# Output projections: splitting moved into the stage in front, no meeting of engines, and projection products inside the last delta head's scan

## The reference

```python
# layer 0 and 1 of the first network
y_lat = jnp.concatenate([o, fourier_mix(f)], axis=-1) @ w_out      # attention heads and Fourier groups
y_lat = hyena_mixer(...)                                           # (gate * long convolution) @ w_out
x = layer_norm(alpha * x + g1 * y_lat, ln1_g[i], ln1_b[i])
# layer 0 and 1 of the second network
y = o * lax.rsqrt(jnp.mean(o * o, axis=-1, keepdims=True) + EPS) * onorm   # gated delta rule, 8 heads
y_lat = (y.astype(z.dtype) * jax.nn.silu(z).reshape(...)).reshape(b, l, d) @ w_out
y = (gate_b * conv3_grid(gate_c * hx, conv_w, rows)) @ w_out       # short convolution
x = x + gt_m * y
```

## Time and profile before

| | us |
|---|---|
| median of 3 runs (3809.39 to 3812.03) | 3809.65 |
| profiled execution | 3807.93 |
| its span | 3806.0 |
| PE busy / DVE busy / ACT busy / POOL busy | 3340.8 / 1824.8 / 1131.5 / 428.9 |

### The profile page before, as it was taken

How to read it: one execution, slowest core, us unless ns; L and a number is a source line. 1 busy time by engine, 2 the same in 40 slices (tenths; PEclk the granted TensorE clock), 3 DMA queues, 4 the chain that set the end, 5 groups by cost and what they waited for, 6 DMA issues and landing times. The chain is left out here.

```text
span 3806.0 us, 47649 instructions
## 1 busy us (share of the span) xinstructions
PE 3340.8 (88%) x18241; PEld 2257.7 (59%) x18241; DVE 1824.8 (48%) x2900; ACT 1131.5 (30%) x1882; POOL 428.9 (11%) x428
## 2 busy tenths in 40 slices
PE   8999899899988899977999998699886996998886
PEld 6767587766755787746888886344332773433332
DVE  6774687457874877354565564311112543111112
ACT  3042443234213332345445443111111321111111
POOL 1200000001300000012233230111110000111110
PEclk7999999999989999988999998799998997999998
DMA  6340355322612355211121120699997204999995
GB/s 226 130 148 23 102 177 181 133 100 89 243 67 66 122 178 187 68 27 32 32 58 37 32 76 2 261 405 400 425 411 284 108 24 201 415 406 407 401 391 206
DMA packets 224678, 692.89 MB, mean 182 GB/s; under 512 B 28019, under 2 KB 108115, under 8 KB 199284
## 3 DMA queue, kind: packets, MB, share of 16 engines
q1 hardware_dynamic: 194016, 652.63, 45.0%
q10 hardware_dynamic: 11764, 20.97, 1.5%
q0 software_dynamic: 18720, 16.84, 1.3%
HBM read 700.78 MB, written 40.94 MB: 195 GB/s over the span
## 5 line engine op out<-in xcount | busy, mean ns | idle before, releaser
L642 PE MATMUL psum<-work_rounded 128*128 128x512 f32 (+1 forms) x2224 | 811.6, 405 | 76.9 <-DVE work_rounded L636 32.7
L642 PE MATMUL psum<-work_rounded,ring_rounded 128*128 128x512 f32 (+1 forms) x1824 | 726.9, 399 | 0.0
L642 PEld LDWEIGHTS psum<-work_rounded 128*128 128x128 f32 x2224 | 429.2, 193 | 189.6 <-issue 78.7
L3678 PE MATMUL psum<-ring,fixed 128*64 128x512 f32 x1184 | 414.7, 658 | 96.3 <-DMA ring<-in_w 55.0
L631 ACT ACTIVATE work_rounded<-ring 128x1024 fp32r<-128x1024 f32 x204 | 214.3, 1057 | 804.5 <-PE psum L642 665.5
L642 PE MATMUL psum<-fixed_rounded,work_rounded 128*128 128x512 f32 (+1 forms) x1088 | 435.6, 400 | 0.0
L642 PEld LDWEIGHTS psum<-work_rounded,ring_rounded 128*128 128x128 f32 x1824 | 353.2, 194 | 81.1
L3833 DVE TENSOR_TENSOR work<-work,psum 64x512 f32<-64x512 f32 (+1 forms) x64 | 44.2, 691 | 700.0 <-ACT work L3763 546.1
L636 DVE TENSOR_TENSOR ring_rounded<-ring,work_rounded 128x1024 fp32r<-128x1024 f32 x189 | 230.3, 1222 | 274.5 <-ACT work_rounded L631 274.5
L3678 PEld LDWEIGHTS psum<-ring,fixed 128*64 128x64 f32 x1184 | 130.9, 150 | 332.8 <-issue 332.8
L365 DVE SCALAR_TENSOR_TENSOR work<-ring,fixed,work 128x512 f32<-128x512 f32 x364 | 300.6, 835 | 25.5 <-issue 1.7
(11 more groups left out here) (408 smaller groups left out, 5022.2 us busy)
## 6 DMA issues: line engine op xcount, KB each, us to landing
ring<-in_w SPq DMA_DIRECT2D x128, 2048.0 KB, 17.1
work<-in_w SPq DMA_DIRECT2D x64, 2048.0 KB, 21.5
ring<-in_mod_w SPq DMA_DIRECT2D x24, 2048.0 KB, 8.4
ring<-in_ada_w SPq DMA_DIRECT2D x24, 2048.0 KB, 8.1
ring<-in_ffn_w_in SPq DMA_DIRECT2D x44, 1024.0 KB, 7.6
ring<-in_ffn_w_out SPq DMA_DIRECT2D x10, 2048.0 KB, 7.8
ring<-in_w_in_a SPq DMA_DIRECT2D x32, 512.0 KB, 6.6
ring<-in_hy_w_in SPq DMA_DIRECT2D x6, 2048.0 KB, 8.2
```

The lines of the kernel that those rows point to most:

```text
L642: ins = pe.matmul(out, c.rounded(w), c.rounded(x), start=(start and i == 0), stop=(stop and i == 2))
L3678: ins = pe.matmul(c.ps[64 * j:64 * j + 64, 2, :], self.gt_sb[:, k, 0:64], weights(o, j)[:, k, :], start=(k == 0), stop=(k == KD - 1))
```

## The change

The three simple stages and `DeltaHeads` are now joined, so the four barriers go. The splits of the projection stand in the stage in front: on ACT and DVE as the tiles are completed in `FourierMix`, `HyenaConv` and `ShortConv`, and on ACT and POOL in the inversion and scan of delta head 7 (its last tile on ACT and DVE). Split parts have new places, and in the delta projection four units in place of three. In `FourierMix` the turning of the heads is put ahead of the second group, and the tiles are consumed in the order 4, 0, 1, 2, 3, 5, 6, 7. In head 7, products of the output projection stand behind steps 3, 4 and 5 of the scan and around the mean over features, into PSUM banks that are free there. No arithmetic is added or taken away: the number of splits and matmuls is the same.

```diff
@@ class Project
+    def unit_in(self, act, m):
+        if m % 4 == 0:
+            self.c.arrived(act, self.n[m // 4])
+        self.parts.make_high(act, m, self.unit(m), None, 0)
+    def tile_in(self, act, q):
+        act.wait_ge(self.ready, self.ready0 + q + 1)
+        self.parts.lift(act, q)
+    def part_of_tile(self, pe, m, steps):
+        ins = self.parts.product(pe, self.bank(m), m, self.unit(m), steps, True)
@@ Project.scalar
-        c.arrived(act, self.n[0])
-        self.parts.open_high(act, self.unit(0), self.unit(1))
-        for k in range(KD):
-            self.parts.lift(act, k)
-        self.parts.make_high(act, 2, self.unit(2), None, 0)
@@ Project.vector
-        self.parts.open_low(dve, self.unit(0))
-        for k in range(KD):
-            self.parts.lower(dve, k)
-        for m in range(1, UNITS):
-            self.parts.make_low(dve, m, self.unit(m))
@@ FourierMix
-            if g == 2:
+            if g == 1:
                 self.attention.turn(pe)
...
+        project.units_in(act)
+        for g, tiles in enumerate(((0, 1, 2), (3, 4, 5), (6,), (7,))):
...
@@ HyenaConv.scalar, .vector
+            if m in (1, 2, 3):
+                self.project.unit_in(act, m - 1)
+            for q in {4: (0, 1, 2), 5: (3, 4), 6: (5,), 7: (6, 7)}.get(m, ()):
+                self.project.tile_in(act, q)
...
+            for q in {5: (0, 1, 2), 6: (3, 4), 7: (5, 6, 7)}.get(m, ()):
+                parts.lower(dve, q)
@@ ShortConv.vector
+                for q in {22: (0, 1, 2), 23: (3, 4, 5, 6, 7)}.get(j, ()):
+                    parts.lower(dve, q)
@@ DeltaHeads.gpsimd, after the eight heads
+        parts.open_low(pool, project.unit(0))
+        for m in range(1, project.count):
+            parts.make_low(pool, m, project.unit(m))
+        for q in range(DHEADS - 1):
+            parts.lower(pool, q)
@@ DeltaHeads.tensor
-        self.tensor_sums(pe, DHEADS - 1)
+        project.part_of_tile(pe, 1, range(2, last))
+        self.tensor_sums(pe, last)
+        project.part_of_tile(pe, 2, range(0, last))
+        for m in range(3):
+            project.part_of_tile(pe, m, range(last, KD))
@@ DeltaHeads.tensor_scan, at the end of a step
+            else:
+                for m, steps in {3: ((0, range(0, 2)),), 4: ((0, range(2, 5)),), 5: ((0, range(5, 7)), (1, range(0, 2)))}.get(step, ()):
+                    self.project_out.part_of_tile(pe, m, steps)
@@ DeltaHeads.scalar_invert, scalar_scan
+            if h + 1 == DHEADS and v > WHOLE - 2:
+                self.project_out.unit_in(act, v - WHOLE + 1)
...
+            if h + 1 == DHEADS and l and step < 2:
+                self.project_out.unit_in(act, 2 + step)
+            if h + 1 == DHEADS and l:
+                for q in ((0,), (1, 2), (3, 4), (5, 6), (), ())[step]:
+                    self.tile_in(act, q)
@@ stages
-            add(FourierMix(c, attention))
+            mixer = add(FourierMix(c, attention), joined=True)
-            add(HyenaConv(c))
+            mixer = add(HyenaConv(c), joined=True)
-            add(heads)
+            add(heads, joined=True)
-            mixer = add(ShortConv(c))
+            mixer = add(ShortConv(c), joined=True)
```

More of the change, by code:

```diff
@@ L710, in first_two, with product @@
         return last
-    def product(self, pe, out, u, w):
-        self.ready(pe, u)
-        for k in range(KD):
[L715 to L718, removed]
+    def product(self, pe, out, u, w, steps=range(KD), sources=False):
+        if steps[0] == 0:
+            self.ready(pe, u)
+        for q in steps:
+            if u == 0 or sources:
+                self.ready_source(pe, q)
+            k = self.order[q]
+            x, x_high = self.src[q]
+            ins = three(self.c, pe, out, self.unit_high(u)[:, k, :], w[:, k, :], x_high, x, q == 0, q == KD - 1)
         return ins
@@ L726, with __init__ @@
 class Project(Stage):
[L729 removed]
+    def __init__(self, core, w, src, gate, keep, high, units, count=UNITS, order=None, banks=None, signalled=True):
         super().__init__(core)
[L731 removed]
+        self.gate, self.keep, self.count = gate, keep, count
         self.norm, self.leads, self.route = None, True, None
+        self.banks = list(range(KD)) if banks is None else banks
+        self.begun = 0
+        self.ready, self.ready0 = core.shared("x_tile", KD if signalled else 0)
         self.tiles, self.tiles0 = core.shared("x_tile", KD)
@@ L1326, in vector @@
             dve.tensor_tensor(out[:, 0:256], even, self.odds[:, g, :], ALU.add)
-            dve.tensor_tensor(out[:, 256:512], even, self.odds[:, g, :], ALU.subtract)
+            dve.tensor_tensor(out[:, 256:512], even, self.odds[:, g, :], ALU.subtract).then_inc(project.ready, 1)
+        join(0)
+        self.attention.finish(dve, project)
+        parts.open_low(dve, project.unit(0))
+        parts.lower(dve, 0)
+        parts.lower(dve, 1)
+        join(1)
+        parts.make_low(dve, 1, project.unit(1))
+        for q in (2, 3, 4):
+            parts.lower(dve, q)
+        join(2)
+        parts.lower(dve, 5)
+        parts.make_low(dve, 2, project.unit(2))
+        join(3)
+        parts.lower(dve, 6)
+        parts.lower(dve, 7)
 F_ACT = W0
@@ L2619, in scalar, with tile_in @@
         self.deviate_o(act, DHEADS - 1)
+        self.tile_in(act, DHEADS - 1)
+    def tile_in(self, act, h):
+        self.wait(act, h, "mixed", 1)
+        self.project_out.parts.lift(act, h)
     def project(self, pe, h, i, ks):
@@ L4000, in stages @@
             add(DeltaIn(c, l, ffn.ahead, gates, heads), joined=True)
-            add(heads)
+            add(heads, joined=True)
             mix, w = c.mix, d["w_out_a_2"][0]
+            rooms = {"high": heads.spare(), "units": RING0 + SLOT * ((heads.before + 2) % SLOTS), "count": 4,
+                     "banks": [4, 6, 7, 3, 0, 2, 5, 1], "signalled": False}
         else:
```

98 lines of the change are left out of this document (70 added, 28 removed).

## The result

The changed kernel took 3776.61 us (median of 4 runs, 3775.35 to 3782.35), the kernel before beside it 3810.27 (median of 4). The ratio is 0.9919, with a 95% interval of 0.9908 to 0.9931: 0.8% faster. The prediction was 3778, with a range of 3772 to 3787.

The account below looks back on a forecast made before the run. PE was taken to bound the kernel, idle at four joints behind DVE's low parts and then slowed by a low clock. 22.83 - 0.5 + 9.4 (13.42 - 4.0) = 31.7 us gained, giving 3778, range 3772 to 3787.

Parts of the forecast that it names:

- Simple joints: Behind FourierMix, HyenaConv and ShortConv: PE's gap and low clock go, gaining 22.83 us, less 0.5 for handovers and drains.
- HyenaConv, 8.62: Joint behind HyenaConv: gain of 5.81 us of PE gap plus 2.81 of low clock.
- Low clock follows idle time: At the four joints: PE's clock falls to 1.2 GHz after standing idle, costing 2.68, 2.81, 2.28 and 1.45 us.
- Delta, available 13.42: Joint behind the delta heads: 10.30 us of PE idle, 0.84 of the mean and 2.28 of low clock.
- ACT's split of unit 1: Delta head 7, between L2930 and L2940: one split on the path before the scan costs 1.0 us, bounds 0 to 1.06.
- The lock, 2.0: Delta head 7's scan: DVE's scaling L3126 waits for POOL's operations, costing 2.0 us, bounds 0 to 7.6.
- Clock in the scan, 1.0: Delta head 7: waits in steps 2 and 3 keep PE's clock low, costing 1.0 us, bounds 0 to 5.7.
- Another stage by over 2 us: Sign that the prediction is wrong: a stage other than those named loses or gains more than 2 us.
- nothing is lost in the scan: Rival, delta scan: L3126 does not wait for POOL and the clock recovers; 34.8 us gained, 3775; chance 0.18.
- the scan pays in full: Rival, delta scan: POOL waits and low clock cost 14.3 us, eating the 13.4; 3785 to 3788; chance 0.13.
- a joint still waits: Rival, tiles 3 to 7: PE waits for DVE and low clock stays; 3785 to 3788; chance 0.08.
- does nothing: Rival: PE still meets a late split of unit 0 before every product; 3800 to 3810; chance 0.03.

Follow-up runs that it names:

- splits-late kernel: Changed kernel, no meetings, but splits of the three simple projections made at the projection's own start: 3790.14 us (median of 4), ratio 0.9953 to the kernel before.
- early splits: Changed kernel with ACT's high parts of units 0 and 1 one inversion round earlier in delta head 7: 94.48 us in the delta stretch, 3768.57 in one run.

## Why the prediction was right, step by step

- *Simple joints, 22.83 - 0.5 = 22.3.* Measured 7.56 + 7.64 + 7.12 = 22.3. The margins of 0.5 to 2 us held, PE never waited for a tile. That the sum is exact is luck in part, since it hides an error each way: FourierMix and ShortConv gained 0.2 and 0.3 more, HyenaConv 1.0 less.
- *HyenaConv, 8.62, got 7.64.* The step that failed is to count gap and low clock alone, as if the projection's matmuls kept their pace: seven triples of matmuls took 4.76 us before (0.680 each), six took 4.16 after (0.693 each). Over 64 triples that is 0.86 of the missing 0.98. PE's rows of the kernel before, then of the changed one:

```profile
1192.08 0.39 PE L642 MATMUL psum<-work_rounded,ring_rounded 128*128 128x512 f32 x1
1192.31 0.62 PE L642 MATMUL psum<-work_rounded 128*128 128x512 f32 x2
...
1196.84 0.40 PE L642 MATMUL psum<-work_rounded,ring_rounded 128*128 128x512 f32 x1
```

```profile
1179.48 0.39 PE L642 MATMUL psum<-work_rounded,ring_rounded 128*128 128x512 f32 x1
1179.71 0.62 PE L642 MATMUL psum<-work_rounded,fixed_rounded 128*128 128x512 f32 x2
...
1183.64 0.40 PE L642 MATMUL psum<-work_rounded,ring_rounded 128*128 128x512 f32 x1
```

  The units' high parts moved from `work` to `fixed` memory. Whether the area or the distance to the other operand sets the pace stays open; ShortConv's triples, all in `work` and `ring`, kept their pace (0.682 on average before and after), but the delta projection's, there too, took 0.693 and 0.700 in the two profiles before, and 0.698 after.
- *Low clock follows idle time.* Right for what the kernel before does, and not a rule: the splits-late kernel stood 2.76 and 3.70 us with the clock full behind. The 6.9 us of clock at the simple joints were real, and were saved because no gap is left, not because each gap must cost them.
- *Delta, available 13.42.* The mean met no wait and the tail's thin margin held: L2780 to the last low part took 5.4 us where 5.7 were free. There was more to be had: in the kernel before, the clock was low over the scan's steps 1 and 2 (2297.7 to 2304.5), which took 4.08 and 3.81 us against 3.20 for the next, 1.5 in all. The early splits save these too.
- *ACT's split of unit 1, 1.0.* The wait was 0.97. But its bounds, 0 to 1.06, were wrong: moving it gave 3.5, since the clock stayed full too. That was priced separately, and only for waits in steps 2 and 3.
- *The lock, 2.0.* The waits were 1.48 + 0.55 = 2.03. That they meet the forecast is luck in part: it counted six of the ten operations at some 0.3 us each, and three were held, each for longer, since POOL had its pauses in the scan's first steps and was done by 2303.4. Their price on the path was less. From one L2863 to the next, step 2 took 5.05 us against 3.81 before, with the clock low for 2.9 and 2.7 of it; step 3 without its six products (1.39) took 3.68 against 3.20, at full clock in both. That makes 1.7, and at full clock throughout it was 1.2. PE's rows of the kernel before, then of the changed one (steps 2 and 3 lie between their three starts):

```profile
2301.86 1.22 PE L2772 MATMUL psum<-work 128*128 128x128 f32 x4
...
2305.67 0.42 PE L2772 MATMUL psum<-work 128*128 128x128 f32 x2
...
2308.87 0.42 PE L2772 MATMUL psum<-work 128*128 128x128 f32 x2
```

```profile
2292.67 1.23 PE L2863 MATMUL psum<-work 128*128 128x128 f32 x4
...
2297.72 0.42 PE L2863 MATMUL psum<-work 128*128 128x128 f32 x2
...
2302.79 0.60 PE L2863 MATMUL psum<-work 128*128 128x128 f32 x4
```

- *Clock in the scan, 1.0.* The changed kernel's clock fell between 2285 and 2286, at the scan's first products and before any lock; counted from the scan's first product (2285.68, and 2295.49 before), that is 2.6 us earlier than in the kernel before (about 2297.7). The scan's step 0, up to the first L2863, therefore took 2.91 against 2.29: 0.6, at another place than steps 2 and 3, where the forecast had it. Of 13.42 us 10.08 were got, so all costs were 3.3 and not 4.0: 0.97 the split, 1.7 the lock and 0.6 the clock, where the text had 1.0, 2.0 and 1.0. All three terms were there, two of them somewhat too large. This is the first pair of profiles; in the second the low clock lasts into step 3 (steps 2 and 3 take 5.36 and 5.42), and lock and clock can't be told apart.
- *Another stage by over 2 us.* This did happen. From HyenaConv's end to head 7, before took 1064.8 and 1064.6, after 1067.1 and 1065.8, and the edited kernels 1065.0 to 1068.2; behind ShortConv 2.3 were gained in the first pair. No instruction was changed there. The clock goes with the first of these: it was low for 78.5 us between HyenaConv's end and head 7 in both profiles before, and for 85.3 to 92.2 in the eleven profiles of the changed kernel and its edits, which all took longer there than either profile before. So a part of this loss seems to belong to the change; why the clock is low for longer there is not shown. The sum put every stage outside the joints at nothing, and by its own sign that step failed: in the first pair they lost 1.1, 1.0 and 2.4 us before the delta joint and gained 1.7 and 2.3 behind it. That only 0.5 is left is luck.

The time alone does not tell the forecast from its nearest rival: 3776.61 lies 1.4 us from 3778 and 1.6 from 3775. The stretch does. The rivals "nothing is lost in the scan" (13.4 - 1.0 = 12.4 at this joint) and "the scan pays in full" (-0.9) lie 2.3 and 11 us from the measured 10.1; "a joint still waits" and "does nothing" are ruled out by the joints' rows.

## What to carry to other kernels

A meeting of engines and late splits cover each other: take away both or expect a part (17.9 and 12.6 of 22.3 us here). When work is put into another engine's chain, look for the place where that engine waits anyway; one microsecond at the wrong one cost 3.5. Judge terms of a microsecond by a stretch of the trace between two fixed rows, which repeated to 0.05 us at the simple joints of the two kernels and to 0.4 at the delta joint, and not by the total, which moves by 7. Profile an edited kernel twice all the same: its stretches moved by up to 1.5 where the clock fell otherwise.

## What the runs showed of the hardware

- A stretch that no edit touched, from the norm at 887 us (L431) to HyenaConv's L2103, took 238.1 and 238.2 us in the changed kernel's two profiles and 237.8 to 238.2 in six others, but 235.0, 232.4, 232.5, 231.4 and 229.8 in others. The granted clock goes with it: 0.91 against 0.94, PE busy 210.28 against 204.48 us with the same 853 matmuls:

```profile
887.10:1125.30 238.20, 210.28 (x853) 161.09 (x852) 192.92 (x261) 60.26 (x78) 47.05 (x22) 0.91 0.45 159
```

```profile
886.70:1119.10 232.40, 204.48 (x853) 157.19 (x852) 190.97 (x261) 60.27 (x78) 47.45 (x22) 0.94 0.46 163
```

  (the changed kernel, and that with the early splits, whose edit comes a thousand microseconds later). Up to 8 us of one run's time can be this, whatever the edit.
- DVE's scaling of 128 columns out of work memory waited until POOL's running operation was over (a pair 2.19 us against 0.54 to 0.71), the one out of PSUM with two factors did not (0.73 to 0.84), and costs 0.41 in place of 0.29 alone.
- Three matmuls of 512 columns took 0.680 or 0.693 us at the same granted clock of 1.00 in two kernels that differ there in where the split parts lie.
